# A four-layer transformer kernel: norm turns as products with a diagonal of scales, or as plain transposes of scaled rows

## What is computed

```python
def rms_norm(x, gain):
    xf = x.astype(jnp.float32)
    y = xf * lax.rsqrt(jnp.mean(xf * xf, axis=-1, keepdims=True) + NORM_EPS)
    return (y * gain.astype(jnp.float32)).astype(x.dtype)

h = rms_norm(x, g_pre)
p = h @ w_in
...
y = jnp.concatenate([ya, yb, yc], axis=-1) @ w_out
return x + rms_norm(y, g_post)
```

## Time and profile before

| what | value |
|---|---|
| median of 3 runs | 2170.09 us |
| the three runs | 2145.85, 2170.09, 2173.84 us |
| profiled execution, its span | 2171.3 us |
| TensorE products busy | 2062.2 us (95%), 9552 records |
| TensorE weight loads busy | 1617.0 us, 9552 records |
| VectorE busy | 743.2 us (34%) |
| ScalarE busy | 867.9 us (40%) |
| GpSimd busy | 659.7 us (30%) |
| mean granted clock of TensorE | 0.960 |

### The profile page before, as it was taken

One profiled execution on the slowest core, in us unless ns is written; L12 is line 12 of the kernel. 1 busy time (PEld: TensorE's weight loads), 2 busy tenths in 40 slices (PEclk: granted clock), 3 DMA queues, 4 the chain that ended last, 5 costly groups with the idle time before them and its releaser, 6 DMA issues.

```text
span 2171.3 us, 25579 instructions
## 1 busy us (share of the span) xinstructions
PE 2062.2 (95%) x9552; PEld 1617.0 (74%) x9552; DVE 743.2 (34%) x1278; ACT 867.9 (40%) x1706; POOL 659.7 (30%) x278
## 2 busy tenths in 40 slices
PE   8999999899899999889998998999999999999998
PEld 6866766776777677667767777888878878888886
DVE  3154355324433526551324268111044141111002
ACT  4354455424433535553314355233344343323222
POOL 2422321220232232123202434443310433444442
PEclk9999999999899999899957999999999999999999
DMA  4211211110121121112103222222210232222222
GB/s 141 87 47 61 78 49 40 59 68 20 59 78 59 50 77 59 49 40 78 50 0 117 79 77 79 97 90 92 90 50 4 96 135 78 97 97 97 97 97 88
DMA packets 43755, 157.50 MB, mean 73 GB/s; under 512 B 6144, under 2 KB 6400, under 8 KB 43264
## 3 DMA queue, kind: packets, MB, share of 16 engines
q1 hardware_dynamic: 42640, 148.65, 20.0%
q10 hardware_dynamic: 1008, 7.34, 0.9%
HBM read 151.78 MB, written 4.19 MB: 72 GB/s over the span
## 4 chain that ended last, share of the span: by engine, by line
PE 78%; DVE 13%; ACT 5%; issue 4%; DMA 0%; POOL 0%; DVEq 0%; ACTq 0%; POOLq 0%; SPq 0%
PE bank L574 10%; PE bank L575 10%; PE bank L576 10%; PE bank L577 10%; PE bank L579 10%; PE bank L578 10%; PE bank L664 6%; PE bank L708 5%; DVE probs L1216 3%; PE bank L689 2%; ACT probs L917 1%; DVE probs L1252 1%; PE bank L668 1%; PE bank L673 1%; PE bank L627 1%
## 5 line engine op out<-in xcount | busy, mean ns | idle before, releaser
L557 POOL TENSOR_TENSOR w_hl<-w_raw,w_hl 128x1024 fp32r<-128x1024 f32 x274 | 659.5, 2411 | 1487.3 <-ACT w_hl L783 1486.8
L783 ACT ACTIVATE w_hl<-w_raw 128x1024 fp32r<-128x1024 f32 x274 | 286.9, 1057 | 399.4 <-DMA w_raw<-wstream 398.9
L574 PE MATMUL bank<-act_hl,w_hl 128*128 128x512 f32 x1056 | 433.2, 410 | 2.1 <-DVE act_hl L1106 2.1
L576 PE MATMUL bank<-act_hl,w_hl 128*128 128x512 f32 x1056 | 418.1, 396 | 0.0
L575 PE MATMUL bank<-act_hl,w_hl 128*128 128x512 f32 x1056 | 418.1, 396 | 0.0
L577 PE MATMUL bank<-w_hl,act_hl 128*128 128x512 f32 x672 | 264.8, 394 | 3.4 <-POOL w_hl L557 2.3
L578 PE MATMUL bank<-w_hl,act_hl 128*128 128x512 f32 x672 | 262.9, 391 | 0.0
L579 PE MATMUL bank<-w_hl,act_hl 128*128 128x512 f32 x672 | 262.8, 391 | 0.0
L574 PEld LDWEIGHTS bank<-act_hl,w_hl 128*128 128x128 f32 x1056 | 203.9, 193 | 44.4 <-DVE act_hl L1106 2.6
L576 PEld LDWEIGHTS bank<-act_hl,w_hl 128*128 128x128 f32 x1056 | 202.3, 192 | 44.8
L575 PEld LDWEIGHTS bank<-act_hl,w_hl 128*128 128x128 f32 x1056 | 203.5, 193 | 41.4 <-issue 1.9
(11 more groups left out here) (205 smaller groups left out, 2519.8 us busy)
## 6 DMA issues: line engine op xcount, KB each, us to landing
w_raw<-wstream SPq DMA_DIRECT2D x274, 512.0 KB, 3.4
x_res<-x SPq DMA_DIRECT2D x4, 512.0 KB, 5.6
g_post<-post_gains ACTq DMA_DIRECT2D x4, 512.0 KB, 3.7
x_spill<-x_res ACTq DMA_DIRECT2D x1, 2048.0 KB, 7.2
x_res<-x_spill ACTq DMA_DIRECT2D x1, 2048.0 KB, 8.6
out<-x_res SPq DMA_DIRECT2D x4, 512.0 KB, 2.6
probs<-w_gates ACTq DMA_DIRECT2D x1, 1024.0 KB, 9.3
mask_b<-masks SPq DMA_DIRECT2D x1, 288.0 KB
```

The lines of the kernel that those rows point to most:

```text
L557: nc.gpsimd.tensor_tensor(w_hl[:, slot, 1].rearrange("p c n -> p (c n)"), w_raw[:, slot, :], w_hl[:, slot, 0].rearrange("p c n -> p (c n)" ...
L574: pe.matmul(out_ap, wh, ah, start=start, stop=False)
L576: return pe.matmul(out_ap, wl, ah, start=False, stop=stop)
L783: nc.scalar.activation(w_hl[:, b % RING, 0].rearrange("p c n -> p (c n)"), w_raw[:, b % RING, :], ACT.Copy).then_inc(s_high_done, 1)
```

## The change

VectorE no longer makes a diagonal; it multiplies the whole 128x1024 row tile of x_res by its scale and writes it into y_acc[:, t]. TensorE turns the pieces of y_acc with plain transposes against the identity. Since TensorE now reads the identity and VectorE does not, the wait for s_first moves from VectorE's norm 0 to TensorE's first turn. The semaphores between the engines stay as they are.

```diff
@@ allocations
     y_tok = at("y_tok", [P, 2, TT, P], f32)
-    diag = y_tok[:, 0]
     y_tmp = at("y_tmp", [P, S], f32)
@@ TensorE
             def norm_turn(i, part):
 
+                if i == 0 and part == 0:
+                    pe.wait_ge(s_first, 16 * len(FIRST))
                 for c in NORM_CHUNKS[part]:
...
                     for c in NORM_CHUNKS[part]:
-                        tr = pe.matmul(bank_of(("norm", i, c))[:, t * P:(t + 1) * P], x_res[:, t, c * P:(c + 1) * P],
-                                       diag[:, t, :], start=True, stop=True)
+                        tr = pe.transpose(bank_of(("norm", i, c))[:, t * P:(t + 1) * P], y_acc[:, t, c * P:(c + 1) * P],
+                                          ident[:, :])
@@ VectorE
             def norm_row(i, t):
 
                 dve.wait_ge(s_h_scale, i * TT + t + 1)
-                nc.vector.tensor_scalar(diag[:, t, :], ident[:, :], stat[:, 8 + t:9 + t], None, ALU.mult)\
+                nc.vector.tensor_scalar(y_acc[:, t, :], x_res[:, t, :], stat[:, 8 + t:9 + t], None, ALU.mult)\
                     .then_inc(s_h_rows, 1)
 
             def norm(i):
                 if i == 0:
-                    dve.wait_ge(s_first, 16 * len(FIRST))
                     for t in range(TT):
                         norm_row(0, t)
```

## The result

| | before | after |
|---|---|---|
| median | 2170.85 us (20 runs, 2138.92 to 2204.38) | 2173.86 us (20 runs, 2143.85 to 2176.74) |
| profiled execution, its span | 2171.3 us | 2172.9 us |

The ratio of the times is 1.0089, 95% interval 1.0050 to 1.0129: a little slower, by less than 2%. The forecast was 2167.4, a little faster. The ratio leaves out runs over 1.5% above the fastest of their kernel, and since the times of both kernels stand on levels 28 us apart, that cuts most runs of before with a long stretch at half clock and hardly any of after, so most of the 0.9% is the mix of levels. Level by level the difference is smaller: runs with no long stretch have medians of 2141.8 before (9 of 20) and 2147.2 after (5 of 20), those with one 2172.9 (7) and 2174.8 (14). Near 2200 there are 4 runs of before and none of after; one run of after, 2157.0, lies between the levels.

The account below looks back on a forecast made before the run. TensorE, 78% of the last-ending chain, was taken to bound the kernel; -7.3 (second halves) + 3.3 (posts) + 0 (norm 0) + 1.35 (clock) = -2.65 us from 2170.09 gave 2167.4 us, range 2139 to 2176.

Parts of the forecast that it names:

- Second halves, -7.3: Chunks 4 to 7 of each norm's turn, inside a dense stream: plain transposes save 1.82 us a norm, -7.3 us.
- Scales and posts, +3.3: Three posts: VectorE's longer row scales +1.44, TensorE's shorter first half -0.34, products 1.10 us later each, +3.3 us.
- The addition as a bound: Upper bound for a 128x1024 scale on VectorE: the addition of L1397, 1.23 us, +0.94 a row.
- Norm 0 and GpSimd, zero: Norm 0's first product waits for GpSimd's weights, and GpSimd rests during all four scales: no cost at either.
- Clock, +1.35 behind the first products: After each norm's first product the clock stays low 4.4 us, 2.7 us longer in all, half lost: +1.35 us.
- my bounds: Clock cost behind the four norms' first products, from the shortest and longest low stretch: -1.9 to +1.8 us.
- a matter of chance by this trace: Low-clock stretch at the end of a fox attention, worth up to 29 us, read as chance.
- the change touches nothing there: Claim that the change leaves the attention's low-clock stretch alone; shown runs read as two with one and one without.
- Sum: All terms together, -7.3 + 3.3 + 0 + 1.35 = -2.65 us, giving 2167.4 us.
- The third: Rival: second halves' transposes also drop the clock, 4 x 2.2 = +8.8, sum +6.2, 2176.3 us; chance 0.04.
- The first: Rival: median falls on runs without the low stretch, 2143.2 us, chance 0.31; or with two, 2196, chance 0.05.

Follow-up runs that it names:

- four pairs: After less before in four settings: whole kernel, attention left out, attention tails filled with idle products, all waits filled; the whole moved +1.5, +3.5, +4.5, +3.8 us.
- b1: The kernel before, unchanged, run once more for a second trace: 2173.6 us.
- n5: Changed kernel without attention units, each transpose of the norms' first halves done twice, against the same kernel with them done once: 1636.43 us.
- n6: Changed kernel without attention units, first halves as full products by the identity, against the same kernel with plain transposes there: 1636.81 us.
- e3: The changed kernel itself, run again as a control beside before: median 2174.4 us, ratio 1.006, interval including 1.
- the split: Against before: first halves keep diagonal products; second halves are plain transposes of half rows VectorE scales when it would wait: 2169.3 us, ratio 1.003.
- n2: The changed kernel with all attention units left out, against before cut the same way (1636.93 us): 1639.65 us.
- g3: Before with idle products in attention tails, norms 1 to 3 and recurrence, second halves as transposes of rows scaled in VectorE's idle time: 2141.58 us, ratio to before 0.9929.
- g1: Before with idle products in TensorE's waits at the fox attention tails, ahead of first-half rows of norms 1 to 3 and in the recurrence: 2146.10 us.

## Why the prediction was right and wrong

- **Second halves, -7.3: right.** 3.49 to 1.66 us from start to next product at every norm, 1.83 each.
- **Scales and posts, +3.3: right.** 0.749 us a scale (estimate 0.761); three posts +3.2; VectorE's busy time rose by 7.3 (7.7). The addition as a bound was far too wide: the same operation at two other sizes gave the price.
- **Norm 0 and GpSimd, zero: right.** First product 15.97 against 16.14, in a range of 15.4 to 16.7 over all traces; no scale took over 753 ns, while L1395 took 2.81 as before.
- **Clock, +1.35 behind the first products and nothing anywhere else: this step failed, and it turned the sign.** All that is neither turn nor post came to 5.6, 7.7, 8.6 and 7.3 us in the four pairs, more than the 3.5 to 4.1 that turns and posts save.
- **Its first part, the stretch behind the first products.** I set 4.4 us low at each. In after it was 4.0 (by the distance of the products), 3.3, 3.8 and 5.6, and the excess over full clock 7.9 us against 7.4 before: +0.5, inside my bounds by luck. In the other pairs it was +4.8, +8.7 and +4.1, outside my bounds of -1.9 to +1.8. What I took for a constant of the place isn't one: at norm 0 before was low for 3.0 us and b1, the same kernel, not at all. The way it moves was right: with half as many records of TensorE in the first half the clock comes back later (norm 0, n5, n6). Its size rested on one stretch behind four transposes elsewhere. The prediction said that at the first halves the clock is low either way; with products it is often back before the stream starts, and the one trace of before could not show it.
- **Its second part: the low stretch as "a matter of chance by this trace", and "the change touches nothing there".** Between the norms it was +5.3 in the profiled pair (attention 3.7, recurrence 1.6), which turned the sign there, and +2.3, -1.0 and +3.1 in the others. The third block is slower in all four pairs. The attention's share has no steady sign, and its cause stays open. Two traces of one kernel repeat which layer has the long stretch: before and b1 layer 1, with 568.0 and 567.9 us, after and e3 layer 0, with 569.8 and 568.9 (e3 had a further 27 us low in layer 1, and 551.8 us there against 541.5); two such pairs can be chance. The counts are not: 38 of 144 runs of before are at two long stretches and none of the 30 of after and e3; with one there are 46 and 21. So the change does touch how many there are. The means over all levels are 2168.7 (without the run of 3998) and 2167.3 us, with a standard error of 3 us on the difference, so on average the change is worth nothing that can be told, and the median moves by which level holds the middle.
- **Sum.** Low-clock time on record grew by 14, 18, 17 and 15 us in the four pairs. Half of that, 7 to 9 us, is an estimate of its cost beside the 5.6 to 8.6 above: low time in TensorE's waits costs nothing, and the late start of the record leaves out what after lost at norm 0.
- **From the sum to the median.** 2167.4 was 2171.3 - 2.65 - 1.2. Measured: 2171.3 + 1.6 + 1.0. Of the 6.4 us 4.2 are the sum, and 2.2 come from my taking the median to lie 1.2 below the span, where that of after lies 1.0 above. A run's time is some 2 us above its span (2175.08 and 2172.9 in the profiled run of after), so that 1.2 was only which run was the middle one of three.
- **Rivals.** The third named the clock and gave 2176.3, 2.4 off, but for the wrong place: behind the second halves the clock never fell in after (621.40 on, 1.00). The first gave its level a chance of 0.31, by one shown run in three; in the end 5 of 20 runs of after had no long stretch, and 9 of 20 of before.

## What to carry over

Where TensorE waits at all, a cut of a few us is priced only to within what the clock takes back: measure how long the granted clock is low before and after in more than one trace of each, and take half the difference as an estimate. Compare runs of one level with runs of the same level. Take work off inside dense streams, and leave the work that TensorE has ahead of a stream where it is; put the scaling into time in which VectorE waits (the split). Shorter work in front of a stream can cost more than it saves (n2 against n5 and n6). If runs stand on levels, find the wait where the long stretch begins and fill it before timing anything small.

## What was unexpected of the hardware

- A granted clock of 0.50 lasted 65 us over dense work once it began in a fox tail, and cost 28 us; behind the norms it was back after 3 to 6. What keeps it low for so long was not found.
- The record of the clock begins only where the clock first rises, 10 to 23 us into the span, and a window ahead of that says 1.00. At norm 0 of after the window says 1.00, but the products start 0.43 us apart, as at half clock, until 19.95, and 0.23 apart from then on:

```profile
15.97 0.77 PE L576 MATMUL bank<-w_hl,act_hl 128*128 128x512 f32 x1 [1.90 <-POOL w_hl L556]
16.54 0.63 PE L577 MATMUL bank<-w_hl,act_hl 128*128 128x512 f32 x1
...
20.55 0.39 PE L578 MATMUL bank<-w_hl,act_hl 128*128 128x512 f32 x1
```

```profile
16.00:25.20 9.20, 9.20 (x41) 7.68 (x41) 0.92 (x2) 1.85 (x3) 4.72 (x2) 1.00 0.20 71
```

- An fp32 product of 128x128 is two records and 218 ns of TensorE's time, a plain transpose of the same piece one and 104 ns (3.49 and 1.66 us for 16).
- Doing the transposes of the first halves twice made a kernel faster (n5, 3.2 us), since the clock came back sooner.
- Still open: why g3 lost 2.1 us against g1 in layer 0's attention, at equal time at half clock (34 us in both), why two traces of one kernel put the long stretch in the same layer while its runs spread over levels, and why kernels whose VectorE scales whole rows had no run with two long stretches.
